# Two border edits, one late norm product and one GpSimd fill in a 39,000-instruction kernel

## What is computed

```python
def rms_norm(x, g):
    y = xf * lax.rsqrt(jnp.mean(xf * xf, axis=-1, keepdims=True) + EPS)
    return (y * g.astype(jnp.float32)).astype(x.dtype)
def swiglu(x, w_gu, w_down):
    gate, up = jnp.split(x @ w_gu, 2, axis=-1)
    return (jax.nn.silu(gate) * up) @ w_down
h = h + 0.5 * swiglu(rms_norm_2(h, ffn1_norm[l]), ffn1_w_gu[l], ffn1_w_down[l])
h = h + hybrid_mixer(rms_norm_2(h, mix_norm[l]), w_in[l], ...)
h = h + 0.5 * swiglu(rms_norm_2(h, ffn2_norm[l]), ffn2_w_gu[l], ffn2_w_down[l])
```

## Time and profile before

| | us |
|---|---|
| median of 3 runs | 2855.35 (2850.11 to 2858.96) |
| profiled execution | 2854.27 |
| its span | 2852.5 |
| TensorE busy in it | 2784.5 |
| VectorE, ScalarE, GpSimd busy | 1854.2, 1133.3, 840.8 |

### The profile page before, as it was taken

The page is one execution under the profiler, slowest core; times in us unless marked ns, Lnnn a source line. Parts: engine busy times, 40 slices in busy tenths (PEclk is TensorE's granted clock), DMA queues, the critical chain, the costliest instruction groups (busy, mean ns, idle before and its releaser), DMA issues. The chain is left out here.

```text
span 2852.5 us, 38952 instructions
## 1 busy us (share of the span) xinstructions
PE 2784.5 (98%) x13862; PEld 2374.3 (83%) x13862; DVE 1854.2 (65%) x3223; ACT 1133.3 (40%) x1895; POOL 840.8 (29%) x555
## 2 busy tenths in 40 slices
PE   8999999999999999999999999999999999999998
PEld 6777878888888888899999998888877787788887
DVE  6587565687588888459989896444244676454433
ACT  4324432333366666533333334233132346432222
POOL 0221202445433334468887860000020230000001
PEclk9999999999999999999999999999999999999999
DMA  4221432444445554689999993333353000233332
GB/s 155 76 89 62 157 111 96 141 136 144 144 157 187 178 210 168 231 299 389 392 394 392 391 391 124 104 92 101 96 123 108 30 31 1 96 97 97 96 100 77
DMA packets 187735, 460.94 MB, mean 162 GB/s; under 512 B 28865, under 2 KB 84673, under 8 KB 186434
## 3 DMA queue, kind: packets, MB, share of 16 engines
q1 hardware_dynamic: 160578, 358.21, 38.6%
q0 software_dynamic: 25344, 75.59, 6.8%
q10 hardware_dynamic: 1664, 25.19, 2.2%
HBM read 393.88 MB, written 65.01 MB: 161 GB/s over the span
## 5 line engine op out<-in xcount | busy, mean ns | idle before, releaser
L87 PE MATMUL cb_y<-cb_g_hi,s_hi 128*128 128x368 f32 x1024 | 337.7, 330 | 2.9 <-DVEq L2565 1.8
L88 PE MATMUL cb_y<-cb_g_lo,s_hi 128*128 128x368 f32 x1024 | 337.4, 329 | 0.0
L89 PE MATMUL cb_y<-cb_g_hi,s_lo 128*128 128x368 f32 x1024 | 337.2, 329 | 0.0
L772 POOL TENSOR_TENSOR s_lo<-ex_raw,s_hi 128x1024 fp32r<-128x1024 f32 x96 | 241.9, 2522 | 282.1 <-ACT s_hi L758 282.1
L87 PE MATMUL bs_ps<-x_hi,s_hi 128*128 128x512 f32 x576 | 225.4, 391 | 1.9 <-PEq L2120 1.9
L89 PE MATMUL bs_ps<-x_hi,s_lo 128*128 128x512 f32 x576 | 225.2, 391 | 0.0
L88 PE MATMUL bs_ps<-x_lo,s_hi 128*128 128x512 f32 x576 | 224.9, 390 | 0.0
L2626 POOL DMA_INDIRECT cb_rows<-in_peer_v,ex_chosen x144 | 186.7, 1297 | 66.2 <-issue 42.1
L2621 POOL DMA_INDIRECT cb_units_of<-hidden,ex_chosen x144 | 187.9, 1305 | 54.8 <-issue 42.2
L2588 DVE SCALAR_TENSOR_TENSOR cb_totals<-cb_rows,cb_weight,cb_totals 128x1024 f32<-128x1024 f32 x142 | 182.0, 1282 | 33.2 <-DMA cb_rows<-in_peer_v,ex_chosen 29.5
L87 PEld LDWEIGHTS cb_y<-cb_g_hi,s_hi 128*128 128x128 f32 x1024 | 192.8, 188 | 4.0 <-DVEq L2565 2.2
(11 more groups left out here) (631 smaller groups left out, 7061.8 us busy)
## 6 DMA issues: line engine op xcount, KB each, us to landing
ex_raw<-in_peer_u SPq DMA_DIRECT2D x96, 512.0 KB, 3.7
ex_raw<-in_peer_v SPq DMA_DIRECT2D x96, 512.0 KB
ffn_raw<-in_gu SPq DMA_DIRECT2D x82, 512.0 KB, 3.6
hidden<-up_out SPq DMA_DIRECT2D x128, 256.0 KB, 2.2
routing<-br_out ACTq DMA_DIRECT2D x8, 3072.0 KB, 9.7
cb_route<-routing SPq DMA_DIRECT2D x32, 768.0 KB
cb_unit<-hidden SPq DMA_DIRECT2D x128, 192.0 KB
ffn_raw<-in_down SPq DMA_DIRECT2D x42, 512.0 KB, 3.5
```

The source lines that it names most:

```text
L87: pe.matmul(out, w_high, x_high, start=first, stop=False, skip_group_check=skip)
L88: pe.matmul(out, w_high, x_low, start=False, stop=False, skip_group_check=skip)
L89: return pe.matmul(out, w_low, x_high, start=False, stop=last, skip_group_check=skip)
L772: eng.tensor_tensor(self.lo[:, s, :], self.raw[s], self.hi[:, s, :].bitcast(F32), ALU.subtract).then_inc(self.split, 1)
```

## The change

Four edits. (1) At the borders into ffn1 and into the mixer (p2) four x tiles are split in the stage before, where it was two. (2) In all stages with tiles split ahead, panel 1 is cast behind the last x tile, where it was behind tile 3 (with `ahead` 7 that is no difference). (3) L264 is issued behind panel 2, where it was behind panel 1, in pq, ffn1, p2 and ffn2. (4) The key blocks of the compression are filled on GpSimd, one addition at a time, where VectorE did it; the value blocks stay on VectorE.

```diff
@@ ffn_stage, norm_and_project, project_and_compress: ScalarE and VectorE
-                    if kc == max(3, plain.ahead):
+                    if kc == (KC - 1 if plain.ahead else 3):
                         high_part(act, 1)
@@ ffn_stage, TensorE
                 up(0)
                 up(1)
+                up(2)
                 norm.tensor(pe)
-                for k in range(2, n_up):
+                for k in range(3, n_up):
                     up(k)
@@ norm_and_project, TensorE
-                    if k == 1:
+                    if k == (1 if ring is None else 2):
                         norm.tensor(pe)
@@ project_and_compress, GpSimd
+                pool.wait_ge(S["w"], 16 * 3)
+                pool.wait_ge(S["biases"], 1)
+                fill_blocks(pool, 0, S["pool_blocks"], one_by_one=True)
                 pool.memset(kcT[:], 0.0).then_inc(S["zeros"], 1)
@@ project_and_compress, TensorE
-                        pe.wait_ge(S["blocks"], 16)
+                        pe.wait_ge(S["pool_blocks"], 8)
+                        pe.wait_ge(S["blocks"], 8)
...
-                    if k == 1:
+                    if k == 2:
                         norm.tensor(pe)
@@ project_and_compress, VectorE
                 dve.wait_ge(S["w"], 16 * 3)
-                fill_blocks(0)
                 take(3)
                 low_part(7)
                 take(4)
-                fill_blocks(1)
+                fill_blocks(dve, 1, S["blocks"])
@@ build_program
-        ffn1_plain = Plain(c, "ffn1", hT, gains.of("ffn1_norm"), x_hi, x_lo, 2)
-        mix_plain = Plain(c, "mix", hT, gains.of("mix_norm"), x_hi, x_lo, 2)
+        ffn1_plain = Plain(c, "ffn1", hT, gains.of("ffn1_norm"), x_hi, x_lo, 4)
+        mix_plain = Plain(c, "mix", hT, gains.of("mix_norm"), x_hi, x_lo, 4)
```

More of the change, by code:

```diff
@@ L2826, in project_and_compress @@
             "high", "split", "product", "taken",
-            "w", "hturned", "hidden", "const", "scaling", "biases", "turned", "copied", "gates", "gated", "blocks",
+            "w", "hturned", "hidden", "const", "scaling", "biases", "turned", "copied", "gates", "gated", "blocks", "pool_blocks",
             "part_used", "hid", "gelu", "kc", "kcopied", "scored", "seq", "shifted", "exped", "weights", "pturned", "pcopied",
@@ L2853, in raw_of, with fill_blocks @@
             return raw[:, k % R, :] if k else first.raw[:]
+        def fill_blocks(eng, kv, filled, one_by_one=False):
+            eng.wait_ge(S["taken"], kv + 1)
+            tile = (KCMP, VCMP)[kv]
+            for a in range(2):
+                tokens = proj[:, tile, CMP_STRIDE * a:CMP_STRIDE * (a + NB)]
+                place = pos[:, kv, CMP_STRIDE * a:CMP_STRIDE * (a + 1)]
+                pairs = slice(CMP_STRIDE // 2 * a, CMP_STRIDE // 2 * (a + 1))
+                for odd in range(2):
+                    for g in range(NSA_GROUPS):
+                        part = slice(g * NSA_HD, (g + 1) * NSA_HD)
+                        eng.tensor_tensor(blocks[odd * NSA_HD:(odd + 1) * NSA_HD, kv, pairs, g, :],
+                                          tokens[part].rearrange("p (c r) -> p r c", r=CMP_STRIDE)[:, odd::2, :],
+                                          place[part][:, odd::2].unsqueeze(2).broadcast_to(
+                                              [NSA_HD, CMP_STRIDE // 2, NB]), ALU.add).then_inc(filled, 1)
+                        if one_by_one:
+                            eng.wait_ge(filled, 4 * a + 2 * odd + g + 1)
         with nc.Block() as block:
@@ L3118, in take @@
                         dve.tensor_tensor(place_of(k), bank(k)[:], rstd[:], ALU.mult).then_inc(S["taken"], 1)
[L3120 to L3133, removed]
                 wide = [P, NSA_HEADS, NB]
```

## The result

The changed kernel took 2867.05 us (median of 5 runs, 2856.18 to 2875.0) beside 2855.0 of the kernel before; the ratio is 1.0048 [1.0031, 1.0065]. That is 12 us by the medians, and 14 by the ratio with 9 to 19 as its interval, where 5.2 were forecast. Measured again in another batch it took 2860.62 us beside 2853.97, ratio 1.0039 [1.0022, 1.0056]. Both intervals lie above 1, so it is slower; only the first lies wholly above the 0.3% that a measurement tells from no change. By the medians the second batch gives 6.6 us, so how far the forecast is off depends much on the batch.

What follows compares the result with a forecast made beforehand. TensorE bounds the kernel, with a matmul in flight 2784.5 of 2852.5 us. Terms +3.7 (ffn2) + 1.1 (ffn1) - 2.1 (pq) - 0.9 (p2) + 3.4 (clock) = +5.2 us, so 2860.5 as median; own range 2857 to 2864.

Steps and rivals of the forecast that it cites:

- The chain and the bare gap: ffn1 and ffn2: fixed 7.19 us from L264 to panel 3, TensorE waiting about 6.0 us; ffn2 +3.7 us.
- The border of ffn1: Border into ffn1: with four tiles split ahead, panel 1 starts at 1754.93 instead of 1758.47, 3.5 us gained.
- GpSimd's cover: Ahead of ffn1: two more low parts finish with 0.7 us to spare, cost 0; without the cover 2.56 us.
- The **stage: ffn1, border included: panel 3 at 1773.10 against 1771.97, +1.1 us, with the clock's 1.7 us for a stall counted separately.
- pq: pq stage: L264 no longer waits behind panel 2 and panels 3 and 4 hide the chain, -2.1 us.
- I take 1.7 us for each of the two stalls: ffn1 and ffn2: clock falls behind each 6.0 us gap, +3.4 us together, with 0 and 3.4 as ends for each.
- p: ffn1 and ffn2: clock cost in us of each stall, the change then being +1.8 + 2p.
- the rival on the slower side: Clock stays down behind both ffn stalls: at p = 3.4 it is +8.6 us, 2864 to 2868; chance 0.16.
- 1.8: Whole kernel: the sum with the ffn stalls but no fall of the clock, +5.2 - 3.4, 2857; chance 0.12.
- p2: p2 stage: VectorE's copy at the second transposes comes 0.9 us sooner, not 4.85, since panel 7's load landing stays; -0.9 us.
- the case in which the change makes the loads land sooner: p2: loads issued earlier land sooner, -5.1 in place of -0.9, so +1.0 in all, 2856; chance 0.10.
- the gap at L2942: p2: sign of the forecast being right if still over 3 us, wrong if under 1 us (the landings moved).

Runs made afterwards that it cites:

- e7: Kernel before with the norm product behind panel 2 in both ffn stages, plus 24 unread matmuls filling each gap: 2862.45 us, ratio 1.0028.
- e12: The kernel of e7 run again beside e11, against the kernel before: 2860.38 us, ratio 1.0023.
- e1: Kernel before with one edit, the norm product behind panel 2 in ffn1 and ffn2: 2872.5 us, ratio 1.0061.
- e11: The kernel of e1 run again beside e12, against the kernel before: 2868.79 us, ratio 1.0047.
- e4: Kernel before with one edit, the key blocks of the compression filled on GpSimd: 2854.81 us, ratio 0.9999.
- e2: Changed kernel with the norm product back behind panel 1 in ffn1 and ffn2: 2853.16 us, ratio 0.9992 to the kernel before.
- e8: The changed kernel run again for a second profile, against the kernel before: 2860.62 us, ratio 1.0039.
- e3: Kernel before with the p2 edits (four tiles ahead, norm product behind panel 2, key fills on GpSimd), panel 1's cast also moved in ffn1: 2855.04 us, 0.9999.
- e6: Changed kernel with the ffn norm product back behind panel 1 and panel 3's parts ahead of scale, root and reciprocal: 2852.5 us, 0.9999 to before.
- e10: Kernel before with pq's norm product behind panel 2 and the border of ffn1 (four tiles ahead, panel 1 split behind the last): 2851.12 us, 0.9981.
- e5: Changed kernel with the parts of panels 3 and 4 ahead of scale, root and reciprocal in both ffn stages: 2847.4 us, 0.9976 to before.
- e9: Kernel before with the ffn norm product behind panel 2 and the parts of panels 3 and 4 ahead of scale, root and reciprocal: 2852.34 us, 0.9990.

## Why the forecast fell short

The direction was right, and the place: a fixed chain laid bare in both ffn stages. Its size was not. Step by step:

- **The chain and the bare gap: right.** Forecast 7.19 us from L264 to panel 3, measured 7.11 in both stages, idle 6.09 where "about 6.0" stood, released by L350. With the clock kept up by the filling, ffn2 is 361.1 and 361.2 us: 3.6 and 3.7 over before, where 3.7 was forecast. The two gaps together were put at 3.7 + 4.6 = 8.3, and e7 and e12 cost 8.0 and 6.6. Their ffn1 is longer by 5.9, though, where the gap gives 4.6; in both the clock also fell behind the border gap, where in the profile before it did not (see the last section).
- **The border of ffn1: right**, 3.4 of 3.5 us, and GpSimd's cover held with 0.8 us to spare. The **stage** was put at +1.1 + 1.7 = 2.8 and measured +3.1.
- **pq: right**, -2.3 where -2.1 stood.
- **"I take 1.7 us for each of the two stalls": this step failed.** The price came from one row, behind a gap of 3.39 us. Behind the gap of 6.1 it is more: in the one stretch priced the clock was at 0.50 for 3.4 us, and here it came back 2.9 to 5.9 us into panel 3 (eight gaps, 4.7 on average), which at half the clock is 2.4 us of work. Late against filled, stage by stage: ffn2 363.6 - 361.1 = 2.5 and 363.4 - 361.2 = 2.2; ffn1 3.0 and 2.8. That is 5.2 us for both, where 3.4 stood.

  The runs put it higher: e1 and e7 are 0.0033 apart, e11 and e12 0.0024, or 9.4 and 6.9 us, each uncertain by some 6. The mean granted clock over whole runs points the same way: one minus the clock, times the span, averages 27.3, 27.0, 26.9 and 24.8 us for e1, e11 and the changed kernel twice, and 16.2 to 20.7 us for every kernel without the stalls or with the gap filled. That difference is an upper end, since it counts the low clock inside the gap too, where TensorE had nothing to do (1.2 us between 1772 and 1776 in ffn1).

  So a stall costs 2.6 us in its stage and about 4 by the runs. By the second, p is over the 3.4 from which the rival on the slower side decides, and it did: 1.8 + 2 x 4 = 9.8, beside 12.0 and 6.6 by the medians. With the 2.6 us of the stage alone the sum is 1.8 + 5.2 = 7.0. Both sums lie in the second batch's interval (6 to 16 us), and only the 9.8 in the first's (9 to 19). So that this term was too small is shown; its size is not known better than 5.2 us by the stages and 7 to 9 by the runs.

  The rival's mechanism, a clock that stays down for long behind the stalls, is not what the windows show, though: in the changed kernel it was back 4.2 us into panel 3 of ffn1 and 5.2 us into that of ffn2.
- **p2: -0.9 forecast, nothing found.** The rule for it was that the landing holds the copy, which stands. But the landings scatter: the cast of panel 7 comes 35.6 to 41.9 us into the stage, and the earliest is e7's, whose p2 is untouched. The six profiles with the edits average 135.3 us for p2, the eight others 135.4, with e4, which has the fills alone, among these. The changed kernel itself gave 36.5 and 41.9 in its two profiles. So the 7.1 us of the first profile were chance, and the case in which the change makes the loads land sooner fell. That "the gap at L2942" would be "still over 3 us" failed as a test for the same reason: it was 1.4 in the changed kernel and 3.39 again in e2.
- **The attention: chance, as e8 shows.** Seven of the fourteen profiles have the stage at 186 us or more, with and without each edit, e2, e3 and e6 among them. It adds 6 us to one execution and not to another, a part of why runs of one kernel lie 15 us apart; how many runs have it is not on record. That the edits of p2 make it likelier is not excluded by the profiles (five of the six with them have it, two of the eight without), but the clocks of whole runs speak against it: by the measure above e3 loses 16.2 us, and the 29 runs of before beside it 17.3. The combination's 4 us stand in the first of the changed kernel's two profiles only; in e7's it is 13 us longer than before, without any edit near it.

What stays open: e2, e3 and e6 are 2.3, 0.3 and 0.3 us under before by their ratios, where their stages in the table and pq say 4.7, 2.0 and 6.7 (e3 gains in ffn1 too, since the line that places the cast of panel 1 is in both stages). The intervals of e2 and e3 include the stage sums; that of e6 ends at 4.0. e10 and e5 do show such gains (5.4 where the stages say 4.7, and 6.8 where they say 9.6). For e6 the mean clocks account for 3.9 of the 6.4 us that are missing: its runs lose 20.7 us by them, those of before beside it 16.8, though the first mean is uncertain by 1.6 us. For e2 (18.1 beside 17.3) and e3 (16.2 beside 17.3) they don't, and whether their missing 2 us are the spread of few runs was not settled. The same goes for the part of the clock's price that the ffn stages themselves don't show (1.7 to 4.2 of 6.9 to 9.4 us).

## What to carry to other kernels

Before an instruction is moved later to spare one engine a wait, read the lists of the engines that answer it: here the waits of 2.3 us at L264 and 1.2 us at panel 3 were traded for 12.2 us of gaps, since VectorE kept its next piece of work behind the answer. Moved together with that piece (two low parts ahead of the chain), the same edit takes 2.2 us from ffn2 and 1.5 from ffn1. And a stall on the bounding engine is to be priced with its clock, and by more than one profiled row: filling the gap with matmuls that nobody reads measures that price directly.

## What the runs showed of the hardware

The fall of the clock behind a gap is a matter of chance for gaps near 3 us. The border gap of ffn1, 2.6 to 2.75 us, is untouched in seven profiled kernels. In the kernel before the clock stayed at 1.00 behind it, and in e9; in the five others it fell, in e11 for longest:

```profile
1751.94:1755.94 4.00, 1.31 (x6) 0.74 (x4) 2.14 (x4) 3.01 (x5) 0.00 (x0) 0.91 0.76 279
1755.94:1759.94 4.00, 3.99 (x9) 3.14 (x10) 3.68 (x5) 2.77 (x5) 0.00 (x0) 0.50 0.44 131
1759.94:1763.94 4.00, 4.00 (x15) 3.19 (x14) 3.21 (x5) 3.26 (x6) 0.00 (x0) 0.74 0.41 131
```

So the row on which the forecast rested, a clock that stayed at 1.00 behind 2.63 us, was one draw of two outcomes. What the fall costs depends on what waits behind it: e4 has the ffn stages of the kernel before, and its ffn1 with the fall is 358.4 beside 357.9 without.

Nor does the length of a gap alone tell. TensorE starts the output projection of the mixer (tile `wo_ps`) behind the light work of the attention and a gap of only 1.67 us, shorter than the 2.63 us that did nothing in ffn1, and in all fourteen profiles the clock fell to 0.50 within 1 us of that start. In the kernel before, TensorE's row and the window:

```profile
2437.15 0.49 PE L87 MATMUL wo_ps<-x_hi,first_high 128*128 128x512 f32 x1 [1.67 <-PEq L3325]
...
2436.00:2440.00 4.00, 2.85 (x7) 2.26 (x8) 1.65 (x2) 0.94 (x2) 0.00 (x0) 0.68 0.40 89
```

So a price taken from the row with the nearest length of gap, as the forecast took it, is a rough one.

Behind the gaps of 6.1 us it fell in all eight cases (two stages in four profiles), and never while they were filled. The Trainium skill (TensorE: Matmul & The Clock Gate, HAM oscillation) says that an engine that sits in long idle gaps is throttled and pays for the way back each time; the traces agree, with 2.2 to 3.0 us of stage time for each of these gaps.
